# First projection of a hybrid encoder step: the next pair's weight load issued before two stores, and the last 16 columns' rounded weights and rests in one stationary tile

## The reference, cut to what matters

```
h = rms_norm(x, norm_mix_w) * (1 + sc_m) + sh_m       # x: 1152 tokens x 1024
proj = h @ w_in_ab                                    # w_in_ab: 1024 x 4368
mod = silu(c) @ ada_w[layer] + ada_b[layer]           # c: 9 sequences x 1024, ada_w: 1024 x 6144 per layer
```

## Time and profile before

| | us |
|---|---|
| median of 3 runs (lowest, highest) | 3695.66 (3694.4, 3708.12) |
| the profiled execution, its own time | 3701.06 |
| its span, first to last instruction | 3699.3 |
| TensorE matmul busy (share of the span) | 3471.2 (94%) |
| VectorE, ScalarE, GpSimd busy | 2204.6, 1286.4, 1795.8 |
| mean granted TensorE clock, share of full speed | 0.976 |

### The profile page before, as it was taken

The page is one execution under the profiler, slowest core; times in us unless marked ns, Lnnn a source line. Parts: engine busy times, 40 slices in busy tenths (PEclk is TensorE's granted clock), DMA queues, the critical chain, the costliest instruction groups (busy, mean ns, idle before and its releaser), DMA issues. The chain is left out here.

```text
span 3699.3 us, 69879 instructions
## 1 busy us (share of the span) xinstructions
PE 3471.2 (94%) x29337; PEld 3250.4 (88%) x29337; DVE 2204.6 (60%) x3207; ACT 1286.4 (35%) x2226; POOL 1795.8 (49%) x1388
## 2 busy tenths in 40 slices
PE   7999996999999999999999899989979999999998
PEld 6887875777669899999999899987769899999998
DVE  7656555774885665555544845547766755555446
ACT  5333334663641243333200344435541433332000
POOL 3766653120003377777532378850033677776331
PEclk8999998999999999999999999999989999999999
DMA  6655541101432022222332133333352122223322
GB/s 220 182 180 177 164 159 44 33 23 43 107 100 97 29 65 72 72 72 72 123 94 75 55 123 123 129 125 88 104 150 69 48 72 72 72 72 114 97 88 75
DMA packets 399217, 358.51 MB, mean 97 GB/s; under 512 B 20531, under 2 KB 364113, under 8 KB 393790
## 3 DMA queue, kind: packets, MB, share of 16 engines
q1 hardware_dynamic: 398256, 353.49, 30.0%
q0 software_dynamic: 128, 0.02, 0.2%
q10 hardware_dynamic: 526, 0.60, 0.1%
HBM read 259.40 MB, written 94.68 MB: 96 GB/s over the span
## 5 line engine op out<-in xcount | busy, mean ns | idle before, releaser
L1102 PE MATMUL ffn_acc<-ffn_BH,ffn_WH 128*128 128x384 f32 x1232 | 417.9, 339 | 22.7 <-DVE ffn_BL L1321 12.5
L1102 PE MATMUL ffn_acc<-ffn_BL,ffn_WH 128*128 128x384 f32 x1232 | 416.0, 338 | 0.0
L1102 PE MATMUL ffn_acc<-ffn_BH,ffn_WL 128*128 128x384 f32 x1232 | 415.4, 337 | 0.0
L1037 POOL TENSOR_TENSOR ffn_WL<-raw,ffn_WH 128x512 fp32r<-128x512 f32 x176 | 283.1, 1610 | 259.4 <-ACT ffn_WH L1191 259.4
L2121 PE MATMUL ffn_acc<-ffn_BH,ffn_WH 128*128 128x384 f32 x1056 | 353.7, 335 | 7.1 <-DVE ffn_BL L2185 4.3
L2121 PE MATMUL ffn_acc<-ffn_BL,ffn_WH 128*128 128x384 f32 x1056 | 353.4, 335 | 0.0
L1037 POOL TENSOR_TENSOR ffn_WL<-ffn_S,ffn_WH 128x512 fp32r<-128x512 f32 x176 | 274.6, 1570 | 33.8 <-ACT ffn_WH L1191 33.8
L1102 PEld LDWEIGHTS ffn_acc<-ffn_BH,ffn_WH 128*128 128x128 f32 x1232 | 233.4, 189 | 29.9 <-POOL ffn_WL L1037 14.2
L2194 DVE SCALAR_TENSOR_TENSOR xT<-ffn_acc,mod,xT 128x768 f32<-128x768 f32 x96 | 97.6, 1017 | 254.3 <-PE ffn_acc L2121 254.3
L1102 PE MATMUL ffn_acc<-ffn_hH,ffn_WH 128*128 128x394 f32 x704 | 240.5, 342 | 4.2 <-DVE ffn_hL L1353 3.3
L1102 PE MATMUL ffn_acc<-ffn_hH,ffn_WL 128*128 128x394 f32 x704 | 241.2, 343 | 0.0
(11 more groups left out here) (735 smaller groups left out, 9485.3 us busy)
## 6 DMA issues: line engine op xcount, KB each, us to landing
spare<-in_ada_w SPq DMA_DIRECT2D x42, 1024.0 KB, 7.3
pT<-xT SPq DMA_DIRECT2D x50, 576.0 KB, 3.7
hidden<-ffn_up SPq DMA_DIRECT2D x44, 576.0 KB, 2.8
raw<-in_w_gate SPq DMA_DIRECT2D x44, 512.0 KB, 3.8
raw<-in_w_up SPq DMA_DIRECT2D x44, 512.0 KB, 3.8
raw<-in_w_down SPq DMA_DIRECT2D x80, 256.0 KB, 2.8
raw<-in_w_in_ab SPq DMA_DIRECT2D x34, 512.0 KB, 7.0
raw<-in_w_in_c SPq DMA_DIRECT2D x32, 512.0 KB, 4.1
```

Source lines behind the costliest of these rows:

```text
L1037: self.nc.gpsimd.tensor_tensor(self.WL[:, slot], src, self.WH[:, slot].bitcast(F32), ALU.subtract).then_inc(lo, 1)
L1102: ins = self.nc.tensor.matmul(self.acc[:, bank, 0:n], w[:, slot, k, :], x(low, k), start=start and k == 0 and w is self.WH and low == 0, s ...
```

## The change

In SP's loop `load1` of the next pair moves ahead of both stores, and the second modulation piece moves with it; the store of tile 2j - 2 comes right behind, the store of tile 2j - 1 comes behind the third modulation piece, and `load2` stays last. In the last turn the load of the 16 left-over columns stands where `load1` does.

For these 16 columns GpSimd writes the rests not into `WL` but into columns 32 to 47 of the `WH` tile whose columns 0 to 15 hold the rounded weights. A matmul with 48 stationary columns then gives WH x XH in rows 0 to 15 and WL x XH in rows 32 to 47 of the same PSUM bank; WH x XL has 16 stationary columns as before. VectorE copies rows 32 to 47 out, adds rows 0 to 15, and then weighs the sum. (Columns 16 to 31 hold what was there before; their rows are not read.)

```diff
--- before.py
+++ after.py
@@ -1624,6 +1624,7 @@
         first_rooms = g.spare[:, 0:T], m.middle
         REST_BANKS = (BV, BFAR1, BX)
         rest_cols, rest_bias = cols[0:rest, 1, 0:T], cols[0:rest, 1, T:T + SHIFTS]
+        both, rest_room = 32 + rest, work[0:rest, 1, 0:T + SHIFTS]
 
         def near_of(j, u):
             return (out[:, u, 0:two] if is_gate(j, u) else cols[:, u, HALO:HALO + two])
@@ -1660,15 +1661,15 @@
                 if j == 1:
                     sp.wait_ge(spare_free, 1)
                 later.load(sp, ada, 3 * j - 1)
-                store(2 * j - 2)
                 later.load(sp, ada, 3 * j)
-                store(2 * j - 1)
                 if j + 1 < N:
                     m.load1(sp, j + 1, columns(j + 1, 0))
                 else:
                     sp.wait_ge(m.s3_set, N)
                     sp.dma_start(g.raw[:, 0, :, 0:rest], src[:, :, NAB * P:IN_AB]).then_inc(rest_in, 16)
+                store(2 * j - 2)
                 later.load(sp, ada, 3 * j + 1)
+                store(2 * j - 1)
                 if j + 1 < N:
                     m.load2(sp, j + 1, columns(j + 1, 1))
             sp.wait_ge(later.step_done, later.n)
@@ -1746,7 +1747,7 @@
                 m.pool_group(pool, j, masks_of_pair.get(j))
             for h in range(2):
                 pool.wait_ge(rest_hi, h + 1)
-                nc.gpsimd.tensor_tensor(m.WL[:, 2 + h, :, 0:rest], g.raw[:, 0, h * HALF:(h + 1) * HALF, 0:rest],
+                nc.gpsimd.tensor_tensor(m.WH[:, 2 + h, :, 32:32 + rest], g.raw[:, 0, h * HALF:(h + 1) * HALF, 0:rest],
                                         m.WH[:, 2 + h, :, 0:rest].bitcast(F32), ALU.subtract).then_inc(rest_lo, 1)
             pool.wait_ge(small_in, 64)
 
@@ -1765,11 +1766,11 @@
                 pe.wait_ge((m.c12_done, m.far1_out, m.u3_copied)[c], N)
                 for h, xs in enumerate(halves):
                     for x in xs:
-                        for w, low in ((m.WH, 0), (m.WH, 1), (m.WL, 0)):
+                        for low, wide in ((0, both), (1, rest)):
                             for k in range(HALF):
-                                ins = nc.tensor.matmul(acc[0:rest, bank, 0:n], w[:, 2 + h, k, 0:rest], x(low, h * HALF + k),
-                                                       start=h == 0 and k == 0 and x is xs[0] and w is m.WH and low == 0,
-                                                       stop=h == 1 and k == HALF - 1 and w is m.WL, skip_group_check=True)
+                                ins = nc.tensor.matmul(acc[0:wide, bank, 0:n], m.WH[:, 2 + h, k, 0:wide], x(low, h * HALF + k),
+                                                       start=h == 0 and k == 0 and x is xs[0] and low == 0,
+                                                       stop=h == 1 and k == HALF - 1 and low == 1, skip_group_check=True)
                 ins.then_inc(rest_mm, 1)
 
         @block.scalar
@@ -1983,11 +1984,16 @@
                 far_of(j, 1)
             later.take_mod(dve, 3 * N - 1)
             for c in range(NCH):
+                n = CH + (SHIFTS if c == NCH - 1 else 0)
+                at = slice(c * CH, c * CH + n)
                 dve.wait_ge(rest_mm, c + 1)
-                tt(rest_cols[:, c * CH:(c + 1) * CH], acc[0:rest, REST_BANKS[c], 0:CH], rstd[0:rest, c * CH:(c + 1) * CH],
-                         ALU.mult)
-            nc.vector.tensor_copy(rest_bias, acc[0:rest, REST_BANKS[2], CH:CH + SHIFTS]).then_inc(rest_step, 1)
-            dve.wait_ge(rest_step, 1)
+                nc.vector.tensor_copy(rest_room[:, at], acc[32:both, REST_BANKS[c], 0:n]).then_inc(rest_step, 1)
+                dve.wait_ge(rest_step, 2 * c + 1)
+                tt(rest_room[:, at], rest_room[:, at], acc[0:rest, REST_BANKS[c], 0:n], ALU.add).then_inc(rest_step, 1)
+                dve.wait_ge(rest_step, 2 * c + 2)
+                tt(rest_cols[:, c * CH:(c + 1) * CH], rest_room[:, c * CH:(c + 1) * CH], rstd[0:rest, c * CH:(c + 1) * CH], ALU.mult)
+            nc.vector.tensor_copy(rest_bias, rest_room[:, T:T + SHIFTS]).then_inc(rest_step, 1)
+            dve.wait_ge(rest_step, 2 * NCH + 1)
             nc.vector.tensor_scalar(rest_cols[:, 0:TP], rest_cols[:, 0:TP], rest_bias[:, 0:1], None, ALU.add)
             v = samples(rest_cols)
             tt(v, v, bc(rest_bias[:, 1:SEQS], 2, LS), ALU.add).then_inc(rest_taken, 1)
```

## The result

The changed kernel takes 3667.98 us (median of 5 runs, 3664.88 to 3674.82); the kernel before, beside it, 3700.84 (5 runs, 3694.4 to 3708.12). The ratio is 0.9915, with an interval of 0.9897 to 0.9934: 32.9 us faster where the forecast said 36.3.

The account below looks back on a forecast made before the run. TensorE, busy 94% of the span, bounds the kernel; its stage waits hang on `load1`'s landing. Order -32.5 and tile -3.8 give -36.3 us, from a 3695.66 median to 3659.4, say 3660; range 3651 to 3683.

Parts of the forecast that it names:

- Both waits of TensorE: Groups 6 to 16: TensorE idles 17.5 us for rests of weights and 9.8 us for L1904, before product 2.
- Why it landed late: SP's queue: `load1` lands 10.6 us after issue because a store, 1 MB of modulation weights and another store precede it.
- the upper bound: Groups 2 and 6 to 16: at most 32.2 + 2.0 = 34.2 us can be had; 32.5 taken.
- VectorE's mixes in groups 6 to 9: A mix of some 5 us runs ahead of the addition product 4 waits for; less than 1 us spare.
- What is late next: Later landings on SP's queue and the rests behind them all still hold, with 0.5 to 4 us to spare.
- the held store: Store of tile 2j - 1, moved behind the third modulation piece; from pair 9 ScalarE must await its landing before u3.
- rival (c): Gate pairs: the store of tile 2j - 1 lands over 10.7 us after issue, delaying u3; 3711 us, chance 0.05.
- Nothing is added; four issues change places: SP's loop: moving `load1` ahead of two stores only reorders four issues and adds no work.
- its floor: Group time with TensorE never standing still: 26.72 us with three modulation steps, 26.00 with two and a transpose.
- The tile: 16 left-over columns: 84 matmuls become 56, saving 4.9 us; VectorE's tail adds 1.1; net -3.8.
- Rival (d): Left-over columns: slower 48-column matmuls and a 2 us VectorE tail, 5 us worse than forecast, 3665 us; chance 0.08.
- The port: SBUF port pair: convolution moves beside A21, A11, A12, whose rests come up to 1 us later; S1, S2 become faster.

Follow-up runs that it names:

- Experiment 1: The kernel before with only the new order of SP's loop, the 16 columns as before: 3670.12 us, ratio 0.9915.
- experiment 2: The kernel before with only the 48-column tile for the 16 columns, SP's loop as before: 3696.12 us, ratio 0.9987.
- Experiment 3: The kernel before with only the 1 MB second modulation piece moved ahead of the first store, `load1` still behind both stores: 3676.57 us, ratio 0.9937.
- experiment 5: The changed kernel plus extra 576 KB stores ahead of the store of tile 2j - 1, in turns 10, 11, 12 and 14: 3689.73 us, one run, another chip.

## Why the prediction came out right

**What bounded the stage: right.** Both waits of TensorE had one root, the landing of `load1`. Experiment 1 takes them all away by the order alone, and experiment 2 leaves them all.

**Why it landed late: right, with the shares left open.** I named a store, a megabyte and another store. Experiment 3 gives the shares, but not by its time against experiment 1's, since that one pays for group 3 and this one does not. From where TensorE is ready for group 2 to the stage's last store, the traces have 448.1 us before, 421.3 in experiment 3, and 418.6 in experiment 1, of which 4.7 are group 3's loss. So the megabyte is 26.8 of 34.2 us, and the stores are the rest, in groups 2 and 6 to 10 only.

**The size in groups 2 and 6 to 16: the upper bound came.** I took 32.5 of 34.2, for the sake of VectorE's mixes in groups 6 to 9, where I counted less than 1 us to spare. It was enough: 32.4 + 2.0 = 34.3 came.

**What is late next: the held store, right in kind, and earlier than forecast.** I had the store landing some 9 to 10 us after its issue with 0.9 to 1.9 us to spare for u3 (514.1 to 515.1, wanted at 516.0); it landed at 7.3 with 3.5 spare. The bound of 10.7 us for rival (c) stands: 491.0 - 480.24 = 10.8. The landing of 15.6 us on which the rival rested came from another place, group 3, where no held store is waited for.

**Group 3: missed.** The step that failed is "Nothing is added; four issues change places". I took group 3 as already at its floor, and followed what moved on SP's queue, but not what the earlier `load1` would set off on GpSimd's. Between the rests of A11 and A12 GpSimd issues four small loads there. With `load1` early they start at 132.95 in place of 139.26, 6.3 us earlier, while `load2` moved by only 1.8 us (133.91 to 132.07) and was still under way. That cost 4.7 us. The sign in the earlier trace rows was there: 15.6 us for a store of 576 KB, of which I asked only whether it could happen to a late group, not what had caused it and whether that would move.

**The tile: right in sum.** 28 matmuls of 0.17 are 4.76 us (4.9 forecast): 48 columns cost what 16 do, as I took it (measured -4.75). VectorE's tail grew by 1.18 (1.1). Net -3.6 for -3.8. Rival (d) falls.

**The port.** The convolution moved away from the rests of S1 and S2, as I had worked out, and these went from 4.44 to 2.54 us. But I had it beside the rests of A21, A11 and A12 and these up to 1 us later; in group 15 it runs from 482.68 to 487.08, in a stretch of 7 us in which GpSimd waits for A12, and slows nothing. What I had left out is VectorE's half: its three instructions went from 7.31 to 4.40. That agrees with the rule of the Trainium skill (SBUF — State Buffer, section "SBUF: two separate sides"), by which either engine is blocked while the other holds the pair. None of it reached TensorE, since all of it lies inside waits that had gone.

The sum, by its own terms: forecast -32.5 - 3.8 = -36.3; measured -34.3 + 4.7 - 3.6 = -33.2. The miss is group 3, less the 1.8 us that I had held back. That the total came so near is in part luck: the 1.8 were meant for VectorE's mixes, which needed nothing, and paid for part of a loss that I had not seen.

## What to carry to other kernels

When a load is late, look at what went into its queue right before it: moving one megabyte from in front of it gave nearly four fifths of what the order removed from TensorE's waits here. When a queue's order is changed, ask which DMAs of other engines stand behind something that it makes earlier, the tiny ones above all, and ask of each odd landing in the old trace what caused it: its cause may move onto the path. A store that is held back is safe only up to a landing time that can be worked out beforehand, and it is cheap to force it late once and see.

## What the runs showed of the hardware that was not expected

Four loads of 20 KB in all on GpSimd's queue, in 4-byte and 64-byte pieces spread over the partitions, took 10 to 14 us to land. In the kernel before the 16 DMA engines moved 0 to 1 GB/s in all for about 7 of these. In the changed kernel, where a 512 KB load on SP's queue was under way, they moved 0 to 11 GB/s for 4 us and 27 to 136 for another 5, and that load was read 17.6 us after its issue in place of 8.7.

VectorE's 128x1176 instructions with two SBUF inputs took 2.4 us each beside GpSimd's subtractions and 1.5 us without them; GpSimd's 128x512 subtraction 2.2 and 1.3 us.

The length of a single wait of TensorE does not tell whether the lower clock follows. At the same place in group 3 waits of 3.13 us (experiment 1) and 3.59 us (experiment 5) brought some ten weight loads of 0.33 us in place of 0.19, and 3.76 us (the changed kernel) brought none. In the kernel before 2.48 us ahead of group 11 brought them and 2.88 us ahead of group 16 did not. They can also begin late: behind the 3.27 us of experiment 5 the first load took 0.19 us, and 0.65 us later the loads took 0.30 to 0.33.
